# The up stages of a decoder kernel's feed-forward blocks, by Strassen's scheme

## What is computed

```python
def swiglu(x, w_gate, w_up, w_down):
    return (jax.nn.silu(x @ w_gate) * (x @ w_up)) @ w_down

def half_ffn(x, i, f, j):
    return post_norm(x, 0.5 * swiglu(x, ffn_w_gate[i, f], ffn_w_up[i, f], ffn_w_down[i, f]), i, j)
...
for i in range(DEPTH):
    xp, xs = half_ffn(xp, i, 0, 0), half_ffn(xs, i, 0, 0)
    ...
    xp, xs = half_ffn(xp, i, 1, 2), half_ffn(xs, i, 1, 2)
```

## Time and profile before

| | |
|---|---|
| time, median of 3 runs | 2891.42 us (2889.61 to 2894.22) |
| profiled execution, span from first to last instruction | 2890.1 us |
| PE busy | 2733.8 us, 95% of the span |
| DVE, ACT, POOL busy | 1067.7, 807.7, 663.9 us |
| matmuls | 22548, of them 8448 in the four up stages (44 units x 48 x 4) |
| granted TensorE clock, mean | 0.973 of full speed |

### The profile page before, as it was taken

The page is one execution under the profiler, slowest core; times in us unless marked ns, Lnnn a source line. Parts: engine busy times, 40 slices in busy tenths (PEclk is TensorE's granted clock), DMA queues, the critical chain, the costliest instruction groups (busy, mean ns, idle before and its releaser), DMA issues. The chain is left out here.

```text
span 2890.1 us, 55378 instructions
## 1 busy us (share of the span) xinstructions
PE 2733.8 (95%) x22548; PEld 2607.1 (90%) x22548; DVE 1067.7 (37%) x1707; ACT 807.7 (28%) x1566; POOL 663.9 (23%) x705
## 2 busy tenths in 40 slices
PE   7999998969999998999998999999987998999998
PEld 6999998848999998999998899889986667999997
DVE  2222234555322225222235423544245444422224
ACT  3222212543222213222222422433243222322222
POOL 2222321013322132222321112111211113222231
PEclk9999998989999999999999999999998999999999
DMA  7776734103566654666532134222427993566641
GB/s 248 243 242 221 203 105 111 33 17 129 200 216 216 207 168 141 218 216 211 199 116 80 48 103 129 67 68 68 126 66 263 396 390 108 197 216 216 223 158 45
DMA packets 460502, 478.99 MB, mean 166 GB/s; under 512 B 55886, under 2 KB 433951, under 8 KB 456120
## 3 DMA queue, kind: packets, MB, share of 16 engines
q1 hardware_dynamic: 454880, 464.85, 48.7%
q0 software_dynamic: 5392, 11.67, 1.4%
q10 hardware_dynamic: 64, 0.08, 0.0%
HBM read 463.55 MB, written 198.59 MB: 229 GB/s over the span
## 5 line engine op out<-in xcount | busy, mean ns | idle before, releaser
L737 PE MATMUL bank<-sb_xh,sb_wl 128*128 128x272 f32 x4368 | 944.5, 293 | 52.2 <-DVE sb_wl L1486 27.3
L741 PE MATMUL bank<-sb_xh,sb_wh 128*128 128x272 f32 x4368 | 934.6, 291 | 0.0
L739 PE MATMUL bank<-sb_xl,sb_wh 128*128 128x272 f32 x4368 | 931.3, 290 | 0.0
L1486 DVE TENSOR_TENSOR sb_wl<-sb_raw,sb_wh 128x1024 fp32r<-128x1024 f32 (+1 forms) x337 | 470.4, 1396 | 927.5 <-ACT sb_wh L1219 919.2
L737 PEld LDWEIGHTS bank<-sb_xh,sb_wl 128*128 128x128 f32 x4368 | 705.0, 191 | 59.9 <-DVE sb_wl L1486 30.2
L739 PEld LDWEIGHTS bank<-sb_xl,sb_wh 128*128 128x128 f32 x4368 | 705.2, 191 | 0.6
L741 PEld LDWEIGHTS bank<-sb_xh,sb_wh 128*128 128x128 f32 x4368 | 700.1, 191 | 0.0
L1219 ACT CAST sb_wh<-sb_raw 128x1024 fp32r<-128x1024 f32 (+1 forms) x337 | 374.1, 1111 | 949.0 <-PE bank L741 926.2
L737 PE MATMUL bank<-sb_hh,sb_wl 128*128 128x272 f32 x1408 | 309.2, 291 | 0.0
L739 PE MATMUL bank<-sb_hl,sb_wh 128*128 128x272 f32 x1408 | 304.8, 287 | 0.0
L741 PE MATMUL bank<-sb_hh,sb_wh 128*128 128x272 f32 x1408 | 304.6, 287 | 0.0
(11 more groups left out here) (257 smaller groups left out, 2282.1 us busy)
## 6 DMA issues: line engine op xcount, KB each, us to landing
out_state_b_s<-in_cache_b_kv SPq DMA_DIRECT2D x176, 704.0 KB, 6.3
sb_dkvb<-in_cache_b_kv SPq DMA_DIRECT2D x144, 512.0 KB, 10.3
sb_raw<-in_ffn_w_gate SPq DMA_DIRECT2D x88, 512.0 KB, 3.9
sb_raw<-in_ffn_w_up SPq DMA_DIRECT2D x88, 512.0 KB, 4.4
sb_raw<-in_ffn_w_down SPq DMA_DIRECT2D x64, 704.0 KB, 4.8
sb_raw<-in_attn_b_w_qkv SPq DMA_DIRECT2D x72, 512.0 KB, 3.8
out_state_b_s<-in_cache_b_kv SPq DMA_DIRECT2D x32, 1016.0 KB, 7.8
out_state_b_s<-in_cache_b_kv SPq DMA_DIRECT2D x44, 176.0 KB
```

The source lines that it names most:

```text
L737: pe.matmul(acc(s, h), third(hl, k) if slot == 2 else wl[slot][:, k, :], hi(k)[:, halves[h]], start=start and k == 0, stop=False)
L739: pe.matmul(acc(s, h), third(hh, k) if slot == 2 else wh[slot][:, k, :], lo(k)[:, halves[h]], start=False, stop=False)
L741: last = pe.matmul(acc(s, h), third(hh, k) if slot == 2 else wh[slot][:, k, :], hi(k)[:, halves[h]], start=False, stop=end)
L1486: dve.tensor_tensor(wl[j % 2][:, 0:ph.chunks, :], raw[j][:, 0:ph.chunks, :], v.bitcast(F32), ALU.subtract).then_inc(wl_rdy, 1)
```

## The change

For a group of gate and up weights the product is written as a 2 x 2 block product: the token halves (272 each) are the rows A1, A2, the two halves of the 1024 features are the inner dimension, gate and up are the columns. Strassen's scheme (in Winograd's form) needs seven block products for the eight: a group has 7 x 4 chunks x 3 = 84 matmuls in place of 96. It needs four sums of weight blocks per group (T1 to T4, POOL, `weight_sum`), four sums of token blocks per stage (S1 to S4), and sums of the products behind them (`sum_second`, `sum_third`, `hidden_first`, `gate_second` on DVE, `second_pre` and `hidden_second` on POOL). The weights are split per block of 128 x 512 into a ring of seven slots, so a group has seven splits of 512 in place of two of 1024. The hidden chunks are kept in float32 (`hb`) and are split only when the down stage begins (18 of them on ACT and DVE, 4 on POOL). The raw buffers come free per group: `load_unit` waits for all splits of the group two before. In the first turn of a stage both of the next groups wait for the 13th and 14th split. `scale_x` moves into the loop, two operations behind each of four groups. In the first two groups the products alternate (B11, B11, B21, B21, T1, T1, ...).

```diff
+ORDER = ("B11", "T1", "T2", "B21", "T3", "B22", "T4")
+PAIRED = ("B11", "B21", "T1", "T2", "T3", "B22", "T4")
+RING = 7
+POOL_CHUNKS = 4
...
-                sp.wait_ge(wl_rdy, it * RAW + (ph.u0 + j + 1))
+                if ph.kind == "up" and isinstance(it, int) and it == 1:
+                    sp.wait_ge(wl_rdy, ph.b0 + 2 * RING - 1 + j // 2)
+                elif ph.kind == "up" and not (isinstance(it, int) and it == 0):
+                    sp.wait_ge(wl_rdy, it * (2 * RING) + (ph.b0 + RING * (j // 2) - RING))
...
+            def product(s, g, f, ks=range(QC)):
+                out, (xhi, xlo, c) = product_bank(g, f), left_at[f]
+                for k in ks:
+                    begins, ends = f in ("B11", "T1", "T2", "T4") and k == 0, k == QC - 1
+                    pe.matmul(out, slot_lo(s)[:, k, :], xhi[:, c + k, :], start=begins, stop=False, skip_group_check=True)
+                    pe.matmul(out, slot_hi(s)[:, k, :], xlo[:, c + k, :], start=False, stop=False, skip_group_check=True)
+                    last = pe.matmul(out, slot_hi(s)[:, k, :], xhi[:, c + k, :], start=False, stop=ends, skip_group_check=True)
+                return last
...
+            def group(ph, it, b):
+                ub = FC * ph.ffn
+                for i, f in enumerate(ORDER):
+                    pe.wait_ge(wl_rdy, it * (2 * RING) + (ph.b0 + RING * b + i + 1))
...
+                    elif f == "T3":
+                        pe.wait_ge(p_u2, it * 2 + (ub + b + 1))
...
+                    product(i, b, f).then_inc(mm_done, 1)
...
+            def sum_second(ph, it, b):
+                dve.wait_ge(mm_done, begun(ph, it, b, "T2"))
+                dve.wait_ge(p_v1, it * 2 + (FC * ph.ffn + b + 1))
+                dve.tensor_tensor(u2[b][:], product_bank(b, "T2"), v1[b][:], ALU.add).then_inc(p_u2, 1)
...
+            def group(ph, it, b):
+                next_weight(ph, it, b, "B11")
+                next_weight(ph, it, b, "T1")
+                sum_second(ph, it, b)
+                next_weight(ph, it, b, "T2")
+                next_weight(ph, it, b, "B21")
+                sum_third(ph, it, b)
+                next_weight(ph, it, b, "T3")
+                hidden_first(ph, it, b)
+                next_weight(ph, it, b, "B22")
+                gate_second(ph, it, b)
+                next_weight(ph, it, b, "T4")
...
+            def weight_sum(ph, it, g, f, made):
+                b = g % 2
+                if f == "T1":
+                    for j in (2 * b, 2 * b + 1):
+                        pool.wait_ge(raw_in[j], it * 16 + (ph.land0[j] + 16))
+                pool.wait_ge(t_rdy, it * 8 + made)
+                first, other, how = {"T1": ("B12", "B11", ALU.subtract), "T2": ("T1", "B22", ALU.subtract),
+                                     "T3": ("B22", "B12", ALU.subtract), "T4": ("T2", "B21", ALU.add)}[f]
+                pool.tensor_tensor(weight(g, f), weight(g, first), weight(g, other), how).then_inc(t_rdy, 1)
...
+            def group(ph, it, b):
+                for f in ("T1", "T2", "T3"):
+                    next_sum(ph, it + (b + 1) // 2, (b + 1) % 2, f)
+                second_pre(ph, it, b)
+                next_sum(ph, it + (b + 1) // 2, (b + 1) % 2, "T4")
+                hidden_second(ph, it, b)
...
+            def hidden_second(ph, it, b):
+                ub, h = FC * ph.ffn, hidden_of(it, b)[:, halves[1]]
+                pool.wait_ge(p_c22, it * 2 + (ub + b + 1))
+                pool.wait_ge(sil_1, it * 2 + (ub + b + 1))
+                pool.tensor_tensor(h, h, sil[b][:, halves[1]], ALU.mult).then_inc(hid_1, 1)
```

More of the change, by code:

```diff
@@ new lines, in split, with high_weight @@
+                act.copy(unit_hi(i)[:, 0:ph.chunks, :], raw[j][:, 0:ph.chunks, :]).then_inc(wh_rdy, 1)
+            def high_weight(ph, s, g, f, it=0, b=0):
+                if f in ("B11", "B21", "B22"):
+                    j = 2 * (g % 2) + (f == "B22")
+                    act.wait_ge(raw_in[j], it * 16 + (ph.land0[j] + 16 * (b // 2) + 16))
+                else:
+                    i = 2 * SUMS.index(f) + g if g < 2 else 4 * b + SUMS.index(f)
+                    act.wait_ge(t_rdy, it * 8 + (4 * FC * ph.ffn + i + 1))
+                if isinstance(it, int) and it == 0 and s < RING:
+                    if s in (1, 2):
+                        act.wait_ge(mm_done, ph.b0 - 1)
+                    elif s in (3, 4, 5):
+                        act.wait_ge(mm_done, ph.b0)
+                else:
+                    act.wait_ge(mm_done, it * (2 * RING) + (ph.b0 + s - RING + 1))
+                act.copy(slot_hi(s), weight(g, f)).then_inc(wh_rdy, 1)
@@ new lines, in last_group, with groups @@
+            def last_group(ph):
+                it, nxt = FC // 2 - 1, ph.next
+                keep_first(ph, it, 1)
+                keep_fifth(ph, it, 1)
+                high_hidden(nxt, range(0, 4))
+                gate_first(ph, it, 1)
+                split(nxt, 0)
+                high_hidden(nxt, range(4, 12))
+                gate_second(ph, it, 1)
+                split(nxt, 1)
+                high_hidden(nxt, range(12, FC - POOL_CHUNKS))
+            def groups(ph, n):
+                second_half(ph, n)
+                with act.Fori(1, FC // 2 - 1) as it:
+                    for b in range(2):
+                        group(ph, it, b)
+                group(ph, FC // 2 - 1, 0)
+                last_group(ph)
@@ L1273, in project @@
                     act.wait_ge(norm_ld, 16 * 6 * DEPTH)
-                for i in range(1, ph.units):
-                    split(ph, i, i % RAW, i // RAW)
+                for i in range(2 if down else 1, ph.units):
+                    split(ph, i)
                     if i == (4 if down else 2):
@@ L1467, in _ @@
                 elif ph.kind == "up":
-                    units_ahead(act, ph, split, read)
+                    groups(ph, n_norm - 1 if n_norm else None)
                 else:
@@ new lines, in low_hidden, with last_group @@
+            def low_hidden(ph, ks):
+                for k in ks:
+                    dve.wait_ge(hh_rdy, (FC - POOL_CHUNKS) * ph.ffn + k + 1)
+                    dve.tensor_tensor(hid(hl, k), hid(hb, k), hid_hi(k).bitcast(F32), ALU.subtract).then_inc(hl_rdy, 1)
+            def last_group(ph):
+                it, nxt = FC // 2 - 1, ph.next
+                low_hidden(nxt, range(0, 2))
+                sum_second(ph, it, 1)
+                low_hidden(nxt, range(2, 4))
+                split(nxt, 0)
+                sum_third(ph, it, 1)
+                low_hidden(nxt, range(4, 8))
+                hidden_first(ph, it, 1)
+                low_hidden(nxt, range(8, 12))
+                gate_second(ph, it, 1)
+                split(nxt, 1)
+                low_hidden(nxt, range(12, FC - POOL_CHUNKS))
@@ L1503, in add_tile, with groups @@
+            def groups(ph, n):
+                second_half(ph, n)
+                with dve.Fori(1, FC // 2 - 1) as it:
+                    for b in range(2):
+                        group(ph, it, b)
+                group(ph, FC // 2 - 1, 0)
+                last_group(ph)
             def add_tile(ph, n, m, hs=(0, 1)):
@@ L1816, in _ @@
                 elif ph.kind == "up":
-                    units_ahead(dve, ph, split, read)
+                    groups(ph, n_norm - 1 if n_norm else None)
                 else:
```

722 lines of the change are left out of this document (555 added, 167 removed).

## The result

The changed kernel takes 3041.1 us (median; 3039.6 to 3043.3) beside 2890.5 us of the kernel before: 1.0524 times as long, 95% interval 1.0509 to 1.0539. The forecast said slower, 2943 us; the range ended at 3010. The sum made 52 us of loss, and it is 150. Ratios with an interval are of executions in the faster of two states; one execution of the last version, 5256 us long, is left out of its ratio.

The account below looks back on a forecast made before the run. PE was taken to bound the kernel. Stages two to four lose 41 us together, the first 9.6, attention copies 1: 52 us slower than 2890.1, plus 1.3 outside the span, gives 2943 us; range 2850 to 3010.

Parts of the forecast that it names:

- (g): Down stage's start: first products wait for late chunk splits and their own weights; 2 us lost, between 0 and 6.
- (a): PE's matmuls: 12 of 96 go per group, 10.53 us for 12.03; 132 us over 88 groups if PE kept pace.
- (b): DVE and POOL in the loop block each other by turns: 9.9 us a group if packed, 11.9 by whole operations.
- R3: Rival: in the loop the shared port is held for whole operations; period 11.94 us, 2996 us in all; chance 0.12.
- (c): Loop's dependency chain from T4's end to T3 through sum_second: 0.8 us over PE's cover; period taken as 11.2 us.
- (d): Groups with scale_x, four a stage: two POOL operations on the loop's chain; 12.6 us a group, 14.3 in first stage.
- (e): Start of stages two to four, through the second group: 37.9 us for 23.8, 14 lost; first stage loses 3.
- (f): Second bubble: loads of groups 2 and 3 wait for the 13th and 14th split; 10 us lost a stage.
- The bounds: Whole-kernel time with all terms' bounds on one side: 2801 us on the good side, 3047 on the bad.
- R1: Rival: PE sets the loop's pace, the turns fit into its 0.92 us spare; 2880 us; chance 0.18.
- R2: Rival: stage starts are cheap too, losing 8 us, the bubble 5; 52 us faster, 2839 us; chance 0.17.
- R4: Rival: weight loads are late in every group; about 3015 us if a group lost 1 us; chance 0.05.

Follow-up runs that it names:

- the second experiment: Against the changed kernel, scale_x goes one operation a group over eight groups, behind POOL's sum T4, not two a group over four; 3009.9 us.

## Why the prediction was wrong

The side was right, and all mechanisms but one (g) stood where the forecast put them; every term of the sum came out worse, and the misses added: 30 in the loop, 14 in the groups with `scale_x`, 20 at the starts, 13 in group 2, 25 at the ends, less 4 at the seams.

- **(a) Products.** Right: 0.125 us a matmul at full clock, and 132 us to gain, of which the changed kernel's loop keeps 16. Nothing in the sum priced the clock itself: of the 487 matmuls at half clock 183 lie in the starts, 139 in group 2, 101 in groups 3 to 6 and 64 at the beginning of the down stages, and the forecast counted all of them at full speed.
- **(b) The turns.** The price of one meeting was right on both engines: the split of T1 ended 0.56 us behind POOL's sum (0.54 in the forecast), the sum T3 1.13 behind that split (1.15). The Trainium skill ("SBUF — State Buffer", "Who interferes with whom") calls the shared port pair an exclusive lock and says that a DVE instruction with two SBUF inputs contends with a GpSimd one that reads SBUF; these rows agree up to the last 0.12 to 0.16 us of a whole operation (0.68 and 1.29). The period of 11.7 looks like R3's 11.94, but it is not R3: the same instructions take 10.9 a group in another order.
- **(c) The chain.** Right in every link. The step that failed is the size of the loop's term, the period of 11.2; measured 11.7, so 16 gained for 46. The links themselves gave 11.3, and 11.2 was taken. From the end of T4 to T3 the trace has 6.99 us (mean of groups 8 to 19), the sum 6.8: `gate_second` starts 1.06 us behind T4 for 0.8, the sum T1 takes 1.54 for 1.29 because it meets the split of B11 in every second group (1.78), the split of T1 1.44 for 1.34; the handovers take 0.26 for 0.53, and the 0.25 that was meant for B11's split shows only in that sum T1. And of the 6.02 of its four products PE has 5.85 left at the end of T4, whose last matmul ends 0.16 behind the next one's start. That there was a second chain behind the first, the ring, was not seen at all; it would have held the period at 11.3 even with the first one gone.
- **(d) `scale_x`.** On the chain, as forecast, and the second experiment shows it; at 13.5 a group for 12.6 (15.3 for 14.3 in the first stage). The 11.7 plus two operations is 13.1, and one of the two meets the split of B11: it takes 1.15 to 1.25 us for 0.72.
- **(e) The start.** DVE's row is the bound, as forecast: 36.2 us in the sum, 39.4 in the trace (from 1202.8 to the last of the 14 splits, 1242.2). To the second group's end 41.8 to 43.6 for 37.9, and before 24.5, not 23.8: the second group of a stage was taken at the steady 12.03 and takes 12.75. The turns were mis-sized, not misplaced; which of them cost more than priced is not shown. The first stage was the guess of the sum: 9.3 for 3.
- **(f) Group 2.** 13.4 for 10, near the value that the text gave for a copy in between, and SP's rows show that copy. But the number is partly luck: with the loads 13 us earlier only 5 to 6 of it went. The place of `sum_second`, which the text named as the second wait, held 3.7 more (17.2 to 13.5 when it was moved).
- **(g) The ends.** The step "the last two groups have no sums behind them: PE's 10.53", with 2 us for the down stage, failed outright. The low parts and the down units' splits stand in the queue of the last group itself: a loss of 5 a stage for 1. Four of those 5 went with the new order and two chunks moved off POOL.
- The bounds: all on the bad side gave 3047. The range was cut to 3010, as if not all terms would miss to the same side; all did. In the loop, the groups with `scale_x`, the starts and the ends the experiments show the same two queues, DVE's and POOL's, behind them.

R1, R2 and R4 are excluded for this kernel: PE doesn't set the pace in the loop, the starts are not cheap, and the steady part shows no wait for a load.

## What to carry to other kernels

Where a change takes work from the bounding engine and gives small operations to two others, list for each operation of the new loop who is queued behind it, follow that list once round, and look for a ring; the busy share of the helpers tells little of it (57% and 38% of the span here, 80% and 67% of the loop). Moving two instructions in their queues gave 93 us, and no arithmetic changed. Price the seams with the same care as the loop: a start that costs 17 us takes back 1.2 us of each of the 14 groups that gain.
